# One hybrid decoder layer on eight cores: sums of squares ahead of the first products, fewer fp32 sums for the second group, the pool weight fold spread out

## The reference

```
hn = rmsnorm(x, norm1_g);  proj = einsum('btd,de->bte', hn, w_in)       # D = 1024, w_in 1024 x 2048
u, bg, cg, hc = proj in four parts of 512
d = causal_mean(u, window 2, 4, 8, 16 by channel group) - u
ya = einsum('btgc,gcd->btgd', d, pool_w) * pool_scale                  # four 128 x 128 blocks
yb = bg * conv3(cg * hc)
x = x + einsum('bte,ed->btd', concat(ya, yb), w_out)
hn = rmsnorm(x, norm2_g);  a = relu(hn @ w1);  x = x + (a * a) @ w2     # width 4096
y = rmsnorm(x, final_g)
```

## Time and profile before

| | |
|---|---|
| time, 3 runs | 670.9 us median, 670.86 to 671.53 |
| profiled execution | 670.35 us, span of its slowest core (core 2) 668.2 us |
| spans of the 8 cores | 665.5 to 668.2 us |
| mean granted TensorE clock of a core | 0.995 to 0.998 |
| PE busy | 652.9 us, 98% of the span |
| DVE, ACT, POOL busy | 297.3, 262.8, 75.3 us |

### The profile page before, as it was taken

The page is one execution under the profiler, slowest core; times in us unless marked ns, Lnnn a source line. Parts: engine busy times, 40 slices in busy tenths (PEclk is TensorE's granted clock), DMA queues, the critical chain, the costliest instruction groups (busy, mean ns, idle before and its releaser), DMA issues.

```text
span 667.7 us, 9805 instructions; the slowest of 8 cores (665.5 to 668.2 us)
## 1 busy us (share of the span) xinstructions
PE 652.9 (98%) x3775; PEld 361.8 (54%) x3776; DVE 297.3 (45%) x423; ACT 262.8 (39%) x384; POOL 75.3 (11%) x82
## 2 busy tenths in 40 slices
PE   6999999999999999999999999999999999999996
PEld 4444554555656555565655556565455555555575
DVE  3589787988888402111121221112112111254586
ACT  3533626452446341333324223431431243445265
POOL 7012102300114000000000000000000000303302
PEclk9999999999999999999999999999999999999998
DMA  8996400001939930042340006152000000020215
GB/s 165 235 175 171 174 1 1 0 1 34 114 49 152 167 61 0 1 74 54 56 70 1 1 0 106 22 80 47 0 1 1 1 0 1 1 111 0 115 71 226
DMA packets 12285, 42.49 MB, mean 64 GB/s; under 512 B 3280, under 2 KB 5328, under 8 KB 9552
## 3 DMA queue, kind: packets, MB, share of 16 engines
q0 software_dynamic: 4960, 26.87, 23.7%
q1 hardware_dynamic: 6848, 14.39, 6.2%
q10 hardware_dynamic: 432, 0.61, 0.3%
HBM read 55.69 MB, written 9.24 MB: 97 GB/s over the span
## 4 chain that ended last, share of the span: by engine, by line
PE 95%; DMA 2%; DVE 1%; POOL 0%; issue 0%; ACT 0%; DVEq 0%; POOLq 0%; ACTq 0%
PE psall L661 92%; PE psall L683 2%; DMA big<-win 2%; PE psall L583 1%; PE psall L574 1%; POOL big L470 0%; DVE big L589 0%; PE psall L847 0%; DVE big L1043 0%; PE psall L1034 0%; DVE big L698 0%; DVE big L749 0%; ACT big L544 0%; ACT big L1024 0%; POOL big L1027 0%
## 5 line engine op out<-in xcount | busy, mean ns | idle before, releaser
L661 PE MATMUL psall<-big 128*128 128x464 bf16 (+3 forms) x3584 | 619.4, 335 | 0.0
L661 PEld LDWEIGHTS psall<-big 128*128 128x128 bf16 x3584 | 341.7, 98 | 276.1 <-issue 1.4
L836 DVE TENSOR_TENSOR big<-psall,big 128x896 f32<-128x896 f32 (+2 forms) x96 | 100.6, 1048 | 308.0 <-PE psall L661 307.9
L941 ACT ACTIVATE big<-psall 128x896 f32<-128x896 f32 (+3 forms) x84 | 70.6, 840 | 244.2 <-PE psall L661 243.8
L544 ACT ACTIVATE big<-big 128x928 f32<-128x928 f32 (+3 forms) x64 | 54.9, 863 | 66.3 <-DVE big L836 29.9
L948 ACT ACTIVATE big<-big 128x896 bf16<-128x896 f32 (+3 forms) x79 | 69.6, 881 | 7.0
L589 DVE SCALAR_TENSOR_TENSOR big<-big,psall 128x464 bf16<-128x464 f32 (+4 forms) x96 | 57.9, 651 | 2.3 <-ACT psall L522 2.0
L554 POOL TENSOR_TENSOR big<-big 128x928 f32<-128x928 f32 (+2 forms) x13 | 26.9, 2070 | 191.1 <-ACT big L544 176.2
L772 DVE SCALAR_TENSOR_TENSOR big<-big 128x448 f32<-128x448 f32 (+3 forms) x48 | 28.1, 630 | 2.5 <-ACT big L769 2.1
L554 DVE TENSOR_TENSOR big<-big 128x896 f32<-128x896 f32 (+2 forms) x23 | 23.6, 1025 | 6.3 <-ACT big L544 5.9
L857 POOL DMA_DIRECT2D big<-w x8 | 4.4, 546 | 173.9 <-PE psall L661 173.8
(11 more groups left out here) (53 smaller groups left out, 162.1 us busy)
## 6 DMA issues: line engine op xcount, KB each, us to landing
big<-w POOLq DMA_DIRECT2D x16, 1024.0 KB, 14.2
big<-x POOLq DMA_DIRECT2D x8, 464.0 KB, 11.7
y<-big SPq DMA_DIRECT2D x8, 464.0 KB, 2.9
y<-big SPq DMA_DIRECT2D x8, 448.0 KB, 2.8
big<-win POOLq DMA_DIRECT2D x8, 256.0 KB, 16.6
big<-win POOLq DMA_DIRECT2D x4, 512.0 KB, 30.7
big<-wout POOLq DMA_DIRECT2D x2, 1024.0 KB, 46.2
big<-x SPq DMA_DIRECT2D x1, 1856.0 KB, 15.9
```

The source lines that it names most:

```text
L661: P.add("tensor", lambda e, k=k, i=i: e.matmul(out=PSP[b][:, t, 0:n], lhsT=lhs(k), rhs=rhs(k), start=(i == 0), stop=(i == len(ks) - 1)), r ...
L836: P.add("vector", lambda e: e.tensor_tensor(out=x, in0=PSP[b][:, :, 0:n], in1=x, op=ALU.add), reads=pk(b) + ks, writes=ks, w=2 * n, psum=True)
L941: P.add("scalar", lambda e: e.activation(out=RB[ri][:, :, 0:n], in_=PSP[bk][:, :, 0:n], func=AF.Relu), reads=pk(bk), writes=[("RB", ri)], ...
```

## The change

Four edits, all in the first 75 us:

- For group 0 the four fp32 sums s0 to s3 now all stand ahead of the products u0 to u3, and behind each of them stand 8 matmuls of 128 columns ("k8", `keep_warm`, on a matrix of constants into an unused bank).
- For group 1 the squares of pieces 0, 1 and 2 are added to each other on DVE (two additions of 928 columns, `add_square`), so that two fp32 sums are left of four.
- `W_h` now takes each product out right behind it in the declared order, not after both.
- `fold` is split: the scaling of pool_w stays together (`fold_scale`), and each of the four blocks is multiplied behind one of the products of h and B of group 1.

```
-    def W_h(g):
-        b = [in_mm(g, 2, p) for p in range(2)]
+    def W_h(g, also=()):
         for p in range(2):
-            h_done(g, p, b[p])
-
-    def conv_b(g):
+            h_done(g, p, in_mm(g, 2, p))
+            for q in also[p:p + 1]:
+                fold(q)
+
+    def conv_b(g, also=()):
         for p in range(2):
             conv(g, 2 * p); conv(g, 2 * p + 1)
             b_done(g, p, in_mm(g, 3, p, SKIP[g]))
+            for q in also[p:p + 1]:
+                fold(q)
...
+    def fold(q):
+        b = ps_pair()
+        w = WOUT[:, q, :]
+        P.new_unit()
+        for t in range(2):
+            P.add("tensor", lambda e, t=t: e.matmul(out=PSP[b][:, t, :], lhsT=PWS[:, q, :], rhs=w[:, t * 512:(t + 1) * 512], start=True, stop=True),
+                  reads=[("PWS", q), ("WOUT", q)], writes=[("ps", b, t)], w=512)
+        P.add("scalar", lambda e: e.copy(out=w.rearrange("p (t n) -> p t n", t=2), in_=PSP[b]), reads=pk(b), writes=[("WOUT", q)], w=1024)
...
-    START = ("x0", "x1", "x2", "x3", "s0", "s1", "s2", "u0", "s3", "u1", "u2", "u3"), ("x0", "x1", "x2", "x3", "u0", "u1", "s0", "u2", "s1", "u3", "s2", "s3")
+    FIRST = (("x0", "x1", "x2", "x3", "s0", "k8", "s1", "k8", "s2", "k8", "s3", "k8", "u0", "u1", "u2", "u3"),
+             ("x0", "x1", "x2", "x3", "u0", "u1", "u2", "s0", "u3", "s3"))
     for g in range(2):
         f, sb = norm1(g), st_bank()
         ub, step = in_mm_streamed(g, 0)
-        for what in START[g]:
+        for what in FIRST[g]:
             j = int(what[1])
             if what[0] == "x":
-                x_piece(f, j)
+                x_piece(f, j, g == 0 or j == 3)
+                if g == 1 and j in (1, 2):
+                    add_square(f, 0, j)
+                    if j == 2:
+                        add_halves(f, 0)
+            elif what[0] == "k":
+                keep_warm(j)
...
-    W_h(1)
-    fold()
-    conv_b(1)
+    fold_scale()
+    W_h(1, (0, 1))
+    conv_b(1, (2, 3))
```

More of the change, by code:

```diff
@@ L836, in add_x, with fold_scale @@
         P.add("vector", lambda e: e.tensor_tensor(out=x, in0=PSP[b][:, :, 0:n], in1=x, op=ALU.add), reads=pk(b) + ks, writes=ks, w=2 * n, psum=True)
-    def fold():
+    def fold_scale():
         for q in range(4):
@@ L866, in build_nc, with x_piece @@
     keep_warm(60)
-    def x_piece(f, j):
+    def x_piece(f, j, halves=True):
         f.scale_g(2 * j)
@@ L871, in x_piece, with add_halves, add_square, piece_sum @@
         t, kt = SQ4[j]
-        sq = t[:, :, 0:f.n]
-        f.square(j, sq, kt)
-        P.add("vector", lambda e: e.tensor_tensor(out=sq[:, 0, :], in0=sq[:, 0, :], in1=sq[:, 1, :], op=ALU.add),
-              reads=[kt], writes=[kt], w=f.n)
-    def piece_sum(f, j, b):
+        f.square(j, t[:, :, 0:f.n], kt)
+        if halves:
+            add_halves(f, j)
+    def add_halves(f, j):
+        t, kt = SQ4[j]
+        P.add("vector", lambda e: e.tensor_tensor(out=t[:, 0, 0:f.n], in0=t[:, 0, 0:f.n], in1=t[:, 1, 0:f.n], op=ALU.add),
+              reads=[kt], writes=[kt], w=f.n)
+    def add_square(f, i, j):
+        (t, kt), (v, kv) = SQ4[i], SQ4[j]
+        P.add("vector", lambda e: e.tensor_tensor(out=t[:, :, 0:f.n], in0=t[:, :, 0:f.n], in1=v[:, :, 0:f.n], op=ALU.add),
+              reads=[kt, kv], writes=[kt], w=2 * f.n)
+    def piece_sum(f, j, b, first, last):
         t, kt = SQ4[j]
-        f.mm32(b, [(t[:, 0, 0:f.n], kt)], j == 0, j == 3)
+        f.mm32(b, [(t[:, 0, 0:f.n], kt)], first, last)
     SQ4 = ((SQ[0], ("SQ", 0)), (SQ[1], ("SQ", 1)), (ACC, ("ACC",)), (CV, ("CV", 0, 0, 0)))
-    START = ("x0", "x1", "x2", "x3", "s0", "s1", "s2", "u0", "s3", "u1", "u2", "u3"), ("x0", "x1", "x2", "x3", "u0", "u1", "s0", "u2", "s1", "u3", "s2", "s3")
+    FIRST = (("x0", "x1", "x2", "x3", "s0", "k8", "s1", "k8", "s2", "k8", "s3", "k8", "u0", "u1", "u2", "u3"),
+             ("x0", "x1", "x2", "x3", "u0", "u1", "u2", "s0", "u3", "s3"))
     for g in range(2):
@@ L886, in build_nc @@
         ub, step = in_mm_streamed(g, 0)
-        for what in START[g]:
+        for what in FIRST[g]:
             j = int(what[1])
             if what[0] == "x":
-                x_piece(f, j)
+                x_piece(f, j, g == 0 or j == 3)
[5 more added lines that the diff above has]
+                keep_warm(j)
             elif what[0] == "s":
-                piece_sum(f, j, sb)
+                piece_sum(f, j, sb, j == 0, j == 3)
             else:
```

## The result

The changed kernel takes 674.4 us (median) where the kernel before, run beside it, takes 670.8: ratio 1.0059, 95% interval 1.0044 to 1.0074, slower by about 4 us. Executions in which the cores of one die ran at a lower granted clock, two of nine here and one of nine before, are left out of these medians and of all ratios. The forecast was 671.6 with a range up to 673.3. The profiled execution took 675.4 us, 1.1 more than the median, and that of the kernel before 670.4, so the two profiles differ by more (5.1 us) than the two kernels do.

The account below looks back on a forecast made before the run. PE, busy 98%, was taken as the bound, with the opening setting the slowest core's time; 3.3 us gained there against 4.2 lost at the folds made +0.9, so 671.6 us, range 668.9 to 673.3.

Parts of the forecast that it names:

- third rival: At fold 3's wait, PE's clock falls and costs 1.6 us, giving 673.2 us; chance 0.25.
- C: Start of PE's long run of line 661, behind the opening: forecast 31.1 us, where it was 34.38.
- O(0): End of the changed stretch, behind the folds: forecast to start in effect 44.4 us after line 661's long run, before 40.2.
- The opening: Sums and first products, up to line 661's long run: fewer sums in PE's path and full clock, 3.3 us earlier.
- The waits: PE's new stops at fold 0, second h product, fold 3 and behind it: 1.65, 0.6, 2.8, 0.3 us; 5.35 in all.
- POOL's hold: POOL additions beside DVE instructions with two SBUF inputs delay DVE: 2.45 us in three overlaps.
- rival 1: In the folds, POOL's additions find gaps and DVE isn't held: 669.2 us; chance 0.17.
- The pair order: At the folds, each fold needs the PSUM pair of the B or h half before last, which DVE must have emptied.
- rival 2: At the folds, waits at the pairs don't appear, as DVE has the B results out by then: 666.3 us; chance 0.08.

Follow-up runs that it names:

- The warming matmuls: Changed kernel with 18 warming matmuls ahead of fold 0 and 30 ahead of fold 3, into an unused PSUM bank: 1.0031 to the kernel before.
- own banks: Changed kernel with the four folds in the two PSUM banks of the sums, taking no pair from the products: 0.9945 to the kernel before.
- either order: Folds in the sums' banks, every engine's instructions fixed in the changed kernel's order, 1.0001, or in the order planned for those banks, 0.9945, to the kernel before.
- run with POOL late: Changed kernel with one more wait: POOL's lines 650 and 639 start only after DVE's last line 780 ahead of its first line 792: 1.0023 to the kernel before.
- the pairs in order B: Changed kernel, folds still in the products' PSUM pairs, every engine's instructions in the order planned for folds in the sums' banks: 1.0021 to the kernel before.

## Why the prediction was wrong

**The step that failed is the third rival**: "The clock falls in the wait at fold 3", chance 0.25, price one fall of 1.6 us, put at nothing in the forecast's own sum. Its row was one fall behind 2.3 us without a matmul. It was the likeliest case: six of the eight cores lost their clock at a fold. It came behind 1.8 us of wait too (fold 0, cores 5 and 6), so there were two places for it, and the slowest core took both: 2.5 us by C to O(0), 2.4 by the spans of cores 6 and 7, whose waits and last store are equal. The warming matmuls give 1.9 us back. The prediction saw that eight cores take their chance and the slowest counts, and yet gave it 0.25 and priced a single fall. The Trainium skill, "TensorE: Matmul & The Clock Gate", section "Part 1: The HAM clock gate", has the clock at half rate after idleness; the windows agree with 0.51 behind fold 3, and the equal waits of cores 6 and 7 show that the length of the wait alone did not decide it here.

**The opening was right but for its size**, with C at 31.1 to 31.6 (31.1 forecast) on seven cores. It came 2.8 us earlier on the slowest core where 3.3 were booked: 0.5 off. One reading in it was wrong, without weight for the sum: the 85 ns of a warming matmul are a mean over the first 60 of the program. Those ahead of the folds take 56 ns, each with a weight load of its own, so the loads are not what made the 85.

**The waits were right**: 1.65, 0.6, 2.8 and 0.3 were forecast, 5.35 in all; core 7 shows 1.79, 0.30, 2.90 and 0.30, 5.29. What the sum lacked is that a stop costs more than the idle time that the profile lists for it. That begins at the end of the last matmul's row, and two folds last 0.59 us in their row where the next product otherwise starts after 0.43. C to O(0) grew by 4.9, not 5.3 - 1.1 = 4.2. On core 7 from fold 0's start to the next product pass 0.89 us (61.27 to 62.16), without a stop 0.43 (60.59 to 61.02 with own banks): 0.46 are lost where the row lists 0.30. That is 0.16 more, and at four stops 0.7 in all.

**POOL's hold was right**, and rival 1 falls: 2.45 us were booked for three overlaps; 1.63 us are measured on the six lines 772, and 0.9 on one later line 772, which took 1.60 against 0.70 (core 2, 72.64). The run with POOL late shows it as a cause. The Trainium skill, "SBUF — State Buffer", section "Who interferes with whom", has a DVE instruction with two SBUF inputs shut out for the whole of a POOL instruction that started first, and one with a single SBUF input not; the trace agrees with the second (1.04 us each beside POOL) and with less than the first: 1.63 lost to 2.44 us of POOL.

**The pair order was right, and rival 2 falls**: with banks of their own the waits at the folds are gone in either order. For the slowest core of the profiled execution the sum is then 0.95 forecast, 0.5 less of opening, 0.7 at the stops, 2.5 of clock and 0.9 in the last store, 5.55 of the 5.6. The ratio of the kernels is worth 4.0 us; an estimate for that is the same sum without the store and with the 1.9 us that warming gives back for the clock: 4.05. Why the last store is slow on some cores stays open, and so does why one core's clock falls in a wait in which another's doesn't.

## What to carry to other kernels

A helper product put between others in the same ring of PSUM pairs makes every product behind it wait for a result one place younger; give it a bank of its own before judging where it stands (here the sign of the change turned on it). What two engines share is planned with the order: look at which of the other engine's instructions lie beside the ones that PE waits for. Where a change makes a wait of nearly 3 us in a dense stretch on all cores, count the clock's fall as the likely case for the slowest of them, and once for each such wait: of eight cores five lost it behind 2.9 us in the changed kernel and four with POOL late. Behind 2.0 to 2.1 us it was one of eight in each of two runs, behind 1.8 us two of eight.

## What the runs showed of the hardware that was not expected

- The same wait left the clock up on one core and not on another: 1.79 us ahead of fold 0 on cores 6 (0.58 behind it) and 7 (no fall). At fold 3 of the run with POOL late (2.9 us) four of eight lost it; with the pairs in order B (1.95 and 2.12 us) one of eight.
- Two POOL instructions of 2.44 us together took 1.63 us from six DVE instructions with two SBUF inputs, and themselves ran 1.26 and 1.18 us where, beside lines that read PSUM, they take 1.17 and 0.98.
- A stop of PE costs some 0.16 us more than the idle time that the profile lists for it (0.46 for 0.30, core 7 at the second h product).
